# Feed-forward products of a two-block transformer kernel: two 256-column products of the rounded weights become one of 512 columns

## The chip, the core and the metric

The kernel runs on one core of one Trainium2 chip. The metric is the device time of one execution in microseconds (us), taken as the median of several runs. TensorE (PE), VectorE (DVE), ScalarE (ACT), GpSimd (POOL) and SyncE (SP) each work through a queue of instructions of their own, in order, and wait for each other by semaphores.

## What is computed

A first block of two layers, and a second block with gated recurrences and a mixture of experts. Only the first block's feed-forwards are touched. There are four of them (two in each of two layers), on 256 tokens of width 1024, with 2816 hidden channels:

```python
def rms_norm(x, g, eps=NORM_EPS):
    xf = x.astype(jnp.float32)
    y = xf * lax.rsqrt(jnp.mean(xf * xf, axis=-1, keepdims=True) + eps)
    return (y * g.astype(jnp.float32)).astype(x.dtype)

def swiglu(x, w_gu, w_down):
    g, u = jnp.split(x @ w_gu, 2, axis=-1)
    return (jax.nn.silu(g) * u) @ w_down
...
    for l in range(DEPTH):
        x = x + 0.5 * swiglu(rms_norm(x, ffn1_norm[l]), ffn1_w_gu[l], ffn1_w_down[l])
        x = x + hybrid_mixer(rms_norm(x, mix_norm[l]), ...)
        x = x + 0.5 * swiglu(rms_norm(x, ffn2_norm[l]), ffn2_w_gu[l], ffn2_w_down[l])
```

Everything is float32. A product of float32 precision is made from three products of a shorter format: a matrix is split into a rounded part and the rest (w = wh + wl, x = xh + xl), and w·x is taken as wl·xh + wh·xl + wh·xh. The fourth term is left out.

## The kernel before

Activations lie transposed: channels in the 128 partitions, the 256 tokens (`T`) in the columns. `mm3` (line 284) issues the three products of one pair of 128x128 weights and 128x256 activations into the same 256 columns of PSUM, each with a weight load of its own.

**The up products** (`ffn`, `tensor`): for each of `NFF` = 22 steps n, the gate and the up half (s = 0, 1) of 128 hidden channels, each over `KD` = 8 slices of x: 16 calls of `mm3`, 48 matmuls. Both halves lie in one PSUM bank of 512 columns, taken from a ring of eight. **The down products**: 12 half-jobs of weights of 256 columns (8, 8, 8, 8, 6, 6 slices of the hidden channels, twice), two output blocks each, 176 calls of `mm3`. So a feed-forward makes 352 + 176 calls, 1584 matmuls.

**The weights** come from HBM by SP's queue into a ring of three slots. For each step n ACT rounds a 128x2048 half of a slot (`wh<-RB`, line 423) and DVE subtracts (`wl<-RB,wh`, line 432). `wh` and `wl` have three places each. The loops of ACT and DVE do this for step n + 2 at the top of their iteration n (`ws.high(n + 3)`, `ws.low(n + 3)`), before what they do with the result of step n. `wh` of step m needs the place of step m - 3, so it waits for up(m - 3).

**Behind up(n)**, in the order written by hand:

- DVE, L812: both halves times 1/rms (`RST`), PSUM to SBUF ("scaled");
- ACT, L776: silu of the gate half in place; then L768, the rounding `hh` of step n - 1;
- POOL, L849: silu times the up half ("hidden");
- DVE, L800: `hl`, the rest of step n - 1.

In one iteration DVE does wl(n+2), scaled(n), hl(n-1), and ACT does wh(n+2), silu(n), hh(n-1). At n = 6, 12 and 18 a product for the second block ("ada") follows the up product on PE, and DVE copies its row (`MR`, L758) at the end of the iteration; at n = 7, 13 and 19 PE turns that row. After the down products of four blocks DVE adds them to x (L834).

At the start PE sums the squares after up(0) and ACT and DVE make 1/rms from them, so scaled(0) is late by these steps. The first feed-forward also has some one-time steps: the exponentials of a scalar (with a table load on ACT) at n = 1, and the angles of the rotary embedding on DVE at n = 4 and 6.

Of the kernel before, what the change touches and what calls it, by code (L numbers as in the profile page):

```python
# [15 lines left out]
T = 256  # L16
DM = 1024
KD = 8
# [203 lines left out]
def program(nc, A, out, known):  # L222
    stack = ExitStack()
    with stack:
# [18 lines left out]
        PS = [stack.enter_context(nc.psum_tensor(f"ps{i}", [128, 512], F32))[:] for i in range(8)]  # L243
# [14 lines left out]
        def ps_of(*product):  # L258
            return PS[bank_of[product]]

# [383 lines left out]
        class Head:  # L644
# [3 lines left out]
            def __init__(self, st, g, source, *free):  # L648
                self.st, self.g, self.source, self.free = st, g, source, free
                self.xh, self.xl = sb("xh" + st, X_HIGH, [KD, T], F32R), sb("xl" + st, X_LOW, [KD, T], F32R)  # L650
# [43 lines left out]
        def ffn(f, ws, head, then):  # L694

            st, xh, xl = f"f{f}", head.xh, head.xl
            hh, hl = sb(f"hh{f}", STAGE, [NFF, T], F32R), sb(f"hl{f}", STAGE + 5632, [NFF, T], F32R)
# [3 lines left out]

            def tensor():
                for n in range(NFF):
                    parts = [ws.weights(n)] if n + f else []
                    ps = bank(("up", f, n), ("scaled", f, n))
                    for s in range(2):
                        for k in range(KD):
                            if n + f == 0 and s == 0 and k in (0, 4):
                                parts.append(ws.first(k // 4))
                            hi, lo = parts[k // 4 if n + f == 0 else 0]  # L710
                            j = 2 * k + s if n + f else 2 * (k % 4) + s
                            PE.wait_ge(*at("x_low", st, k))
                            ins = mm3(ps[:, s * T:(s + 1) * T], (hi[:, j, :], lo[:, j, :]),
                                      (xh[:, k, :], xl[:, k, :]), k == 0, k == KD - 1)
# [6 lines left out]
                for g2 in range(2):  # L721
                    bs = [bank(("down", f, 3 * g2 + 2, i // 2, i % 2), ("added", f, 4 * g2 + i)) for i in range(4)]
                    for j, (k0, nk) in enumerate(((0, 8), (8, 8), (16, 6))):
                        for half in range(2):
                            hi, lo = ws.weights(22 + 2 * (3 * g2 + j) + half)
                            for i in range(2):
                                for k in range(nk):
                                    PE.wait_ge(*at("hid_low", f, k0 + k))
                                    ins = mm3(bs[2 * half + i][:, 0:T],
                                              (hi[:, k, 128 * i:128 * i + 128], lo[:, k, 128 * i:128 * i + 128]),  # L730
                                              (hh[:, k0 + k, :], hl[:, k0 + k, :]), k0 + k == 0, k0 + k == NFF - 1)
# [21 lines left out]
            def ada_dve(i, before):  # L753
                if i is not None:
# [3 lines left out]
                    V.tensor_copy(MR, ps_of("ada", i)).then_inc(*did("ada_row", i))  # L758
                if before is not None:
# [5 lines left out]
            def scalar():  # L765
# [31 lines left out]
            def vector():  # L797
# [9 lines left out]
                for n in range(NFF):  # L807
                    ws.low(n + 3)
                    DV.wait_ge(*at("up", f, n))
                    if n >= 4:  # L810
                        DV.wait_ge(*at("hid_low", f, n - 4))
# [10 lines left out]
                    ada_dve(ada_at(f, n), ada_at(f, n - 1))  # L822
                hidden_low(NFF - 1)
                for g2 in range(2):
                    for j in range(3):
                        for half in range(2):
# [3 lines left out]
                            if j == 2:  # L830
                                for i in range(2):
                                    c = 4 * g2 + 2 * half + i
                                    DV.wait_ge(*at("down", f, 3 * g2 + 2, half, i))
                                    V.scalar_tensor_tensor(out=XT[:, c, :],  # L834
                                                           in0=ps_of("down", f, 3 * g2 + 2, half, i)[:, 0:T], scalar=0.5,
# [3030 lines left out]
```

## Time and profile before

| | |
|---|---|
| median of 3 runs | 2518.46 us (2517.13 to 2522.33) |
| the profiled execution, its own time | 2515.94 us |
| its span | 2514.2 us |
| PE busy, share of the span | 2420.3 us, 96% |
| DVE, ACT, POOL busy | 56%, 47%, 12% |
| share of PE in the chain that ended last | 82% |
| granted clock of TensorE, mean | 0.991 of full speed |

The profiled execution lies 2.5 us below the median, and 1.7 us of its time lie around the span. A matmul's duration in the trace reaches over the next one's start, since matmuls are pipelined; what one costs in a stream is the distance of two starts. A row of the timeline has the start (us), the duration (us), engine, line, operation, out<-in and shape, and in brackets the idle time of the engine just before and what ended it.

### The profile page before, as it was taken

The numbers are of one execution on the slowest core, as the hardware profiler recorded it, in microseconds if no ns is written. First come the engines' busy times: TensorE is split into PE (matmuls) and PEld (weight loads), VectorE is DVE, ScalarE is ACT, GpSimd is POOL, SyncE is SP. The second block draws the span as 40 slices with busy tenths as digits, with TensorE's granted clock in tenths as the row PEclk, the third lists the DMA queues.
The fourth block names the chain that finished last, engine by engine and source line by source line (L and its number), as shares of the span: only waits on it lengthen the run. The fifth ranks groups of instructions, "written<-read, shape, count | busy, mean of one in ns | idle before, by whom it ended". The sixth has DMA issues, their size and how long they took to land.

```text
span 2514.2 us, 52384 instructions
## 1 busy us (share of the span) xinstructions
PE 2420.3 (96%) x23215; PEld 2090.9 (83%) x23215; DVE 1408.3 (56%) x2208; ACT 1194.1 (47%) x1725; POOL 296.4 (12%) x417
## 2 busy tenths in 40 slices
PE   7999999999999999999999999899999888999998
PEld 7999888799999998878899995686477767778887
DVE  5655544366646655543666566563434454378886
ACT  5434465444344444474454346431255342277775
POOL 0100000031101100000301000462133222000000
PEclk9999999999999999999999999999999899999999
DMA  8754522266656755422457622101200111379995
GB/s 255 245 207 152 204 89 93 105 202 213 223 184 202 236 183 182 141 99 103 142 194 235 214 74 101 69 4 39 72 32 4 70 37 42 133 245 366 368 364 179
DMA packets 269173, 396.14 MB, mean 158 GB/s; under 512 B 9353, under 2 KB 172862, under 8 KB 268814
## 3 DMA queue, kind: packets, MB, share of 16 engines
q1 hardware_dynamic: 267209, 389.32, 45.2%
q8 instruction: 185, 3.03, 0.5%
q0 software_dynamic: 1120, 2.17, 0.3%
q10 hardware_dynamic: 612, 1.24, 0.1%
q14 instruction: 47, 0.38, 0.0%
HBM read 391.66 MB, written 1.05 MB: 156 GB/s over the span
## 4 chain that ended last, share of the span: by engine, by line
PE 82%; DVE 6%; DMA 6%; ACT 3%; issue 2%; POOL 0%; SPq 0%; ACTq 0%; DVEq 0%; POOLq 0%
PE ps L282 81%; DMA RB<-in_moe_w_up 5%; DVE gwl L432 2%; ACT gwh L423 1%; DVE wl L432 0%; PE ps L1131 0%; ACT wh L423 0%; DVE AR L642 0%; ACT AR L2883 0%; DVE AT L1216 0%; DVE AR L1952 0%; PE ps L526 0%; ACT AR L2875 0%; ACT AT L1185 0%; DMA VR<-in_diff_gain 0%
## 5 line engine op out<-in xcount | busy, mean ns | idle before, releaser
L432 DVE TENSOR_TENSOR wl<-RB,wh 128x2048 fp32r<-128x2048 f32 (+5 forms) x189 | 412.4, 2186 | 283.2 <-ACT wh L423 282.7
L282 PE MATMUL ps<-H,RB 128*128 128x256 f32 (+2 forms) x1728 | 452.8, 421 | 2.8 <-ACT AR L2854 1.3
L423 ACT ACTIVATE wh<-RB 128x2048 fp32r<-128x2048 f32 (+5 forms) x189 | 342.2, 1815 | 230.9 <-PE ps L282 202.7
L282 PEld LDWEIGHTS ps<-H,RB 128*128 128x128 f32 (+1 forms) x1728 | 320.2, 189 | 114.8 <-issue 76.9
L282 PE MATMUL ps<-xhf,wl 128*128 128x256 f32 x1408 | 402.9, 286 | 3.6 <-DVE xlf L671 3.6
L282 PE MATMUL ps<-xlf,wh 128*128 128x256 f32 x1408 | 399.4, 284 | 0.0
L282 PE MATMUL ps<-xhf,wh 128*128 128x256 f32 x1408 | 399.3, 284 | 0.0
L282 PE MATMUL ps<-AR 64*64 64x64 f32 (+3 forms) x8296 | 262.9, 233 | 43.7 <-issue 27.4
L282 PEld LDWEIGHTS ps<-AR 64*64 64x64 f32 (+2 forms) x8296 | 229.2, 140 | 83.2 <-issue 66.0
L282 PEld LDWEIGHTS ps<-xhf,wl 128*128 128x128 f32 x1408 | 271.1, 193 | 14.3 <-issue 10.1
L282 PEld LDWEIGHTS ps<-xlf,wh 128*128 128x128 f32 x1408 | 271.2, 193 | 0.1
L282 PEld LDWEIGHTS ps<-xhf,wh 128*128 128x128 f32 x1408 | 271.2, 193 | 0.0
L432 DVE TENSOR_TENSOR gwl<-RB,gwh 128x2048 fp32r<-128x2048 f32 x96 | 217.3, 2289 | 37.4 <-ACT gwh L423 35.8
L423 ACT ACTIVATE gwh<-RB 128x2048 fp32r<-128x2048 f32 x96 | 183.3, 1925 | 44.3 <-DMA RB<-in_moe_w_up 30.1
L282 PE MATMUL ps<-hh,wl 128*128 128x256 f32 x704 | 199.2, 283 | 0.0
L282 PE MATMUL ps<-hl,wh 128*128 128x256 f32 x704 | 199.2, 283 | 0.0
L282 PE MATMUL ps<-hh,wh 128*128 128x256 f32 x704 | 199.2, 283 | 0.0
L776 ACT ACTIVATE H<-H 128x256 f32<-128x256 f32 x88 | 36.8, 419 | 294.6 <-DVE H L812 294.6
L282 PEld LDWEIGHTS ps<-hh,wl 128*128 128x128 f32 x704 | 135.2, 192 | 0.0
L282 PEld LDWEIGHTS ps<-hl,wh 128*128 128x128 f32 x704 | 135.2, 192 | 0.0
L282 PEld LDWEIGHTS ps<-hh,wh 128*128 128x128 f32 x704 | 135.2, 192 | 0.0
L1452 POOL TENSOR_TENSOR H<-H 128x256 f32<-128x256 f32 x48 | 47.6, 1027 | 683.6 <-DVE H L1423 683.5
(445 smaller groups left out, 4109.0 us busy)
## 6 DMA issues: line engine op xcount, KB each, us to landing
RB<-in_ffn_w_gu SPq DMA_DIRECT2D x88, 1024.0 KB, 7.7
RB<-in_w_in SPq DMA_DIRECT2D x25, 2048.0 KB, 7.8
RB<-in_ffn_w_down SPq DMA_DIRECT2D x16, 2048.0 KB, 7.8
RB<-in_w_gate SPq DMA_DIRECT2D x16, 2048.0 KB, 8.8
RB<-in_moe_w_gate SPq DMA_DIRECT2D x32, 1024.0 KB, 7.6
RB<-in_moe_w_up SPq DMA_DIRECT2D x32, 1024.0 KB, 10.2
RB<-in_moe_w_down SPq DMA_DIRECT2D x32, 1024.0 KB, 8.2
RB<-in_ada_w SPq DMA_DIRECT2D x12, 2048.0 KB, 9.8
```

Source lines behind the costliest of these rows:

```text
L282: return M.matmul(o, lhsT, rhs, start=start, stop=stop, skip_group_check=True)
L423: S.activation(self.pair(h)[0], of(slot_of(*key)), ACT.Copy).then_inc(*did("high", *mark))
L432: V.tensor_tensor(lo, of(slot_of(*key)), hi.bitcast(F32), ALU.subtract).then_inc(*did("low", *mark))
L776: S.activation(sil[:, n % 4, 0, :], sil[:, n % 4, 0, :], ACT.Silu).then_inc(*did("silu", f, n))
L1452: P.tensor_tensor(HB[:, c, :], HB[:, c, :], tmp[:, (8 * i + c) % 4, :], ALU.add).then_inc(*did("merged", l, br, c))
```

## The change

In the feed-forwards, the two parts of x (and of the hidden channels) lie side by side, [xh | xl], 512 columns for each slice. The three products become two: one of 512 columns past wh, giving wh·xh and wh·xl in the two halves of a bank, and one of 256 columns past wl, added into the right half (wl·xh). The small terms so stand in a bank half of their own, and are added at the end. An up step now needs a pair of banks. The last two output blocks of the down products (second group, second half) stay as they were. So 352 + 132 of the 528 calls in a feed-forward change, 1936 in all four.

On ACT a copy of the two right halves to SBUF is new ("rest"); on DVE the old operation L812 is replaced by two: the addition of the left halves and the copy ("summed"), and the multiplication by 1/rms in SBUF ("scaled"). Their order in an iteration also changes. For the down products DVE adds the right half in an operation of its own ("added_rest").

```diff
+        def two_banks(product, *readers):
+            n = bank_at.get(every_bank, 0)
+            n += n % 2
+            bank_at[every_bank] = n + 2
+            for b in (n % 8, n % 8 + 1):
+                for mark in bank_free[b]:
+                    PE.wait_ge(*at(*mark))
+                bank_free[b] = readers
+            bank_of[product] = n % 8
...
+        def mm3_apart(o, w, x, start, stop):
+            wh, wl = w
+            mm(o, wh, x.rearrange("p h n -> p (h n)"), start, False)
+            return mm(o[:, T:2 * T], wl, x[:, 0], False, stop)
...
+            def apart(g2, half):
+                return (g2, half) != (1, 1)
...
-                    ps = bank(("up", f, n), ("scaled", f, n))
+                    two_banks(("up", f, n), ("summed", f, n))
...
-                            ins = mm3(ps[:, s * T:(s + 1) * T], (hi[:, j, :], lo[:, j, :]),
-                                      (xh[:, k, :], xl[:, k, :]), k == 0, k == KD - 1)
+                            ins = mm3_apart(pair_of("up", f, n)[:, s].rearrange("p h n -> p (h n)"), (hi[:, j, :], lo[:, j, :]),
+                                            x[:, k], k == 0, k == KD - 1)
... scalar():
                     ws.high(n + 3)
+                    AC.wait_ge(*at("up", f, n))
+                    if n >= 4:
+                        AC.wait_ge(*at("hid_low", f, n - 4))
+                    S.activation(sil[:, n % 4], pair_of("up", f, n)[:, :, 1], ACT.Copy).then_inc(*did("rest", f, n))
+                    if n:
+                        hidden_high(n - 1)
                     AC.wait_ge(*at("scaled", f, n))
                     S.activation(sil[:, n % 4, 0, :], sil[:, n % 4, 0, :], ACT.Silu).then_inc(*did("silu", f, n))
-                    if n:
-                        hidden_high(n - 1)
... vector():
                     ws.low(n + 3)
-                    DV.wait_ge(*at("up", f, n))
...
-                    V.tensor_tensor(sil[:, n % 4], ps_of("up", f, n).rearrange("p (s n) -> p s n", s=2),
-                                    RST.unsqueeze(1).broadcast_to([128, 2, T]), ALU.mult).then_inc(*did("scaled", f, n))
+                    DV.wait_ge(*at("rest", f, n))
+                    V.tensor_tensor(sil[:, n % 4], pair_of("up", f, n)[:, :, 0], sil[:, n % 4], ALU.add).then_inc(
+                        *did("summed", f, n))
+                    ada_row(ada_at(f, n))
                     if n:
                         hidden_low(n - 1)
+                    DV.wait_ge(*at("summed", f, n))
+                    V.tensor_tensor(sil[:, n % 4], sil[:, n % 4], RST.unsqueeze(1).broadcast_to([128, 2, T]),
+                                    ALU.mult).then_inc(*did("scaled", f, n))
...
+                                    if apart(g2, half):
+                                        V.scalar_tensor_tensor(out=XT[:, c, :], in0=ps[:, T:2 * T], scalar=0.5,
+                                                               in1=XT[:, c, :], op0=ALU.mult,
+                                                               op1=ALU.add).then_inc(*did("added_rest", f, c))
+                                        DV.wait_ge(*at("added_rest", f, c))
```

The order on DVE in the first feed-forward, before, from the copy of the ada row (n = 6) through iterations 7 and 8. L432 is wl(n+2), L812 scaled(n), L800 hl(n-1), L761 the end of the ada step.

```order
61 L758 COPY MR_509<-ps 128x512 [waits s_ada]
62 L432 TENSOR_TENSOR wl_460<-RB,wh_459 128x2048 [waits s_high]
63 L812 TENSOR_TENSOR H<-ps,SM 128x512 [waits s_hid_low,s_up]
64 L800 TENSOR_TENSOR hl_507<-H,hh_506 128x256 [waits s_hid_high]
65 L761 TENSOR_TENSOR SM<-ps,VEC 128x8 [waits s_turned]
66 L432 TENSOR_TENSOR wl_460<-RB,wh_459 128x2048 [waits s_high]
67 L812 TENSOR_TENSOR H<-ps,SM 128x512 [waits s_hid_low,s_up]
68 L800 TENSOR_TENSOR hl_507<-H,hh_506 128x256 [waits s_hid_high]
69 L432 TENSOR_TENSOR wl_460<-RB,wh_459 128x2048 [waits s_high]
```

The same iterations 7 and 8 on DVE after the change. L454 is wl(n+2), L848 summed(n), L838 hl(n-1), L854 scaled(n), L795 the end of the ada step.

```order
69 L454 TENSOR_TENSOR wl_460<-RB,wh_459 128x2048 [waits s_high]
70 L848 TENSOR_TENSOR H<-ps,H 128x512 [waits s_rest]
71 L838 TENSOR_TENSOR hid_504<-H,hid_504 128x256 [waits s_hid_high]
72 L854 TENSOR_TENSOR H<-H,SM 128x512 [waits s_summed]
73 L795 TENSOR_TENSOR SM<-ps,VEC 128x8 [waits s_turned]
74 L454 TENSOR_TENSOR wl_460<-RB,wh_459 128x2048 [waits s_high]
75 L848 TENSOR_TENSOR H<-ps,H 128x512 [waits s_rest]
76 L838 TENSOR_TENSOR hid_504<-H,hid_504 128x256 [waits s_hid_high]
77 L854 TENSOR_TENSOR H<-H,SM 128x512 [waits s_summed]
```

Two operations (L848, L838) now stand between wl and the operation that silu waits for, where none stood before.

The order on ACT, before: L423 is wh(n+2), L776 silu(n), L768 hh(n-1).

```order
54 L423 ACTIVATE wh_459<-RB 128x2048 [waits s_up]
55 L776 ACTIVATE H<-H 128x256 [waits s_scaled]
56 L768 ACTIVATE hh_506<-H 128x256 [waits s_hidden]
57 L423 ACTIVATE wh_459<-RB 128x2048 [waits s_up,s_ring1]
58 L776 ACTIVATE H<-H 128x256 [waits s_scaled]
59 L768 ACTIVATE hh_506<-H 128x256 [waits s_hidden]
```

And after: L445 is wh(n+2), L812 now the new copy "rest"(n), L802 hh(n-1), L816 silu(n), L591 a sine of the first feed-forward.

```order
54 L445 ACTIVATE wh_459<-RB 128x2048
55 L812 ACTIVATE H<-ps 128x512 [waits s_hid_low,s_up]
56 L802 ACTIVATE hid_504<-H 128x256 [waits s_hidden]
57 L816 ACTIVATE H<-H 128x256 [waits s_scaled]
58 L591 ACTIVATE SM<-SM 128x16 [waits s_dve_once]
59 L445 ACTIVATE wh_459<-RB 128x2048 [waits s_ring0]
```

The rounding of step n - 1 has moved from behind silu(n) to ahead of it, and the next wh follows silu directly.

## Rows read from the trace of the kernel before

**Rows 1.** Page, parts 1 and 4: busy time of engines; chain by line.

```profile
PE 2420.3 (96%) x23215; PEld 2090.9 (83%) x23215; DVE 1408.3 (56%) x2208; ACT 1194.1 (47%) x1725; POOL 296.4 (12%) x417
...
PE ps L282 81%; DMA RB<-in_moe_w_up 5%; DVE gwl L432 2%; ACT gwh L423 1%; DVE wl L432 0%; PE ps L1131 0%; ACT wh L423 0%; DVE AR L642 0%; ACT AR L2883 0%; DVE AT L1216 0%; DVE AR L1952 0%; PE ps L526 0%; ACT AR L2875 0%; ACT AT L1185 0%; DMA VR<-in_diff_gain 0%
```

**Rows 2.** Timeline, PE, second feed-forward: first down products, 29 matmuls apart.

```profile
688.43 0.28 PE L282 MATMUL ps<-hh,wl 128*128 128x256 f32 x1
...
691.91 0.28 PE L282 MATMUL ps<-hh,wh 128*128 128x256 f32 x1
```

**Rows 3.** Timeline, PE, projection of 512 columns, 20 matmuls apart.

```profile
259.70 0.39 PE L282 MATMUL ps<-wl,xhp 128*128 128x512 f32 x1
...
264.23 0.39 PE L282 MATMUL ps<-wh,xlp 128*128 128x512 f32 x1
```

**Rows 4.** Timeline, DVE, second feed-forward, iteration 5 and the start of 6.

```profile
588.64 2.29 DVE L432 TENSOR_TENSOR wl<-RB,wh 128x2048 fp32r<-128x2048 f32 x1 [1.05 <-ACT wh L423]
590.85 0.68 DVE L812 TENSOR_TENSOR H<-ps,SM 128x512 f32<-128x512 f32 x1
592.33 0.76 DVE L800 TENSOR_TENSOR hl<-H,hh 128x256 fp32r<-128x256 f32 x1 [0.79 <-ACT hh L768]
594.13 2.29 DVE L432 TENSOR_TENSOR wl<-RB,wh 128x2048 fp32r<-128x2048 f32 x1 [1.04 <-ACT wh L423]
596.34 0.69 DVE L812 TENSOR_TENSOR H<-ps,SM 128x512 f32<-128x512 f32 x1
```

**Rows 5.** Timeline, ACT, the same stretch.

```profile
591.57 0.42 ACT L776 ACTIVATE H<-H 128x256 f32<-128x256 f32 x1 [2.96 <-DVE H L812]
591.89 0.40 ACT L768 ACTIVATE hh<-H 128x256 fp32r<-128x256 f32 x1
592.20 1.90 ACT L423 ACTIVATE wh<-RB 128x2048 fp32r<-128x2048 f32 x1
```

**Rows 6.** Timeline, POOL, the same stretch.

```profile
592.06 0.74 POOL L849 TENSOR_TENSOR H<-H 128x256 f32<-128x256 f32 x1 [4.75 <-ACT H L776]
```

**Rows 7.** Timeline, DVE, second feed-forward, two iterations further on (L812 alone).

```profile
662.67 0.69 DVE L812 TENSOR_TENSOR H<-ps,SM 128x512 f32<-128x512 f32 x1 [0.17 <-PE ps L282]
...
668.42 0.69 DVE L812 TENSOR_TENSOR H<-ps,SM 128x512 f32<-128x512 f32 x1 [0.17 <-PE ps L282]
```

**Rows 8.** Timeline, DVE, second feed-forward: scaled(0), then wl of step 3.

```profile
563.50 0.68 DVE L812 TENSOR_TENSOR H<-ps,SM 128x512 f32<-128x512 f32 x1
566.47 2.29 DVE L432 TENSOR_TENSOR wl<-RB,wh 128x2048 fp32r<-128x2048 f32 x1 [2.29 <-ACT wh L423]
```

**Rows 9.** Timeline, DVE: two operations back to back, three times.

```profile
71.44 0.68 DVE L758 COPY MR<-ps 128x512 f32<-128x512 f32 x1
72.05 2.28 DVE L432 TENSOR_TENSOR wl<-RB,wh 128x2048 fp32r<-128x2048 f32 x1
...
187.18 0.75 DVE L834 SCALAR_TENSOR_TENSOR XT<-ps,XT 128x256 f32<-128x256 f32 x2
```

**Rows 10.** Groups by form, DVE: an operation of 512 columns with SBUF operands only.

```profile
L2948 DVE TENSOR_TENSOR AR<-AR 128x512 f32<-128x512 f32 x8 | 5.5, 683 | 0.0
```

**Rows 11.** Timeline, DVE, the end of the second feed-forward's up part.

```profile
691.08 0.43 DVE L800 TENSOR_TENSOR hl<-H,hh 128x256 fp32r<-128x256 f32 x1 [0.20 <-ACT hh L768]
692.88 2.29 DVE L432 TENSOR_TENSOR wl<-RB,wh 128x2048 fp32r<-128x2048 f32 x1 [1.37 <-ACT wh L423]
```

**Rows 12.** Timeline, ACT, the same place: silu of step 21, then the next wh.

```profile
689.35 0.42 ACT L776 ACTIVATE H<-H 128x256 f32<-128x256 f32 x1 [3.23 <-DVE H L812]
...
690.96 1.89 ACT L423 ACTIVATE wh<-RB 128x2048 fp32r<-128x2048 f32 x1
```

**Rows 13.** Timeline, first feed-forward: wl of steps 3 and 4; first down product.

```profile
34.55 2.29 DVE L432 TENSOR_TENSOR wl<-RB,wh 128x2048 fp32r<-128x2048 f32 x1 [2.29 <-ACT wh L423]
...
41.96 2.29 DVE L432 TENSOR_TENSOR wl<-RB,wh 128x2048 fp32r<-128x2048 f32 x1 [1.59 <-ACT wh L423]
...
159.72 0.28 PE L282 MATMUL ps<-hh,wl 128*128 128x256 f32 x1
```

More of the change, by code:

```diff
@@ L242, in program @@
         EPS = SM[:, 400:402]
-        PS = [stack.enter_context(nc.psum_tensor(f"ps{i}", [128, 512], F32))[:] for i in range(8)]
+        PAIRS_OF_BANKS = [stack.enter_context(nc.psum_tensor(f"ps{i}", [128, 1024], F32))[:] for i in range(4)]
+        PS = [PAIRS_OF_BANKS[i // 2][:, 512 * (i % 2):512 * (i % 2) + 512] for i in range(8)]
         bank_at, bank_free, bank_of = {}, [()] * 8, {}
@@ L259, in ps_of, with pair_of @@
             return PS[bank_of[product]]
+        def two_banks(product, *readers):
[7 more added lines that the diff above has]
+            bank_of[product] = n % 8
+        def pair_of(*product):
+            return PAIRS_OF_BANKS[bank_of[product] // 2].rearrange("p (s h n) -> p s h n", s=2, h=2)
         def view(tensor, col, *dims):
@@ L728, in tensor @@
                                     PE.wait_ge(*at("hid_low", f, k0 + k))
-                                    ins = mm3(bs[2 * half + i][:, 0:T],
-                                              (hi[:, k, 128 * i:128 * i + 128], lo[:, k, 128 * i:128 * i + 128]),
-                                              (hh[:, k0 + k, :], hl[:, k0 + k, :]), k0 + k == 0, k0 + k == NFF - 1)
+                                    w = hi[:, k, 128 * i:128 * i + 128], lo[:, k, 128 * i:128 * i + 128]
+                                    if apart(g2, half):
+                                        ins = mm3_apart(bs[2 * half + i], w, hid[:, k0 + k], k0 + k == 0,
+                                                        k0 + k == NFF - 1)
+                                    else:
+                                        ins = mm3(bs[2 * half + i][:, 0:T], w, (hh[:, k0 + k, :], hl[:, k0 + k, :]),
+                                                  k0 + k == 0, k0 + k == NFF - 1)
                                 ins.then_inc(*did("down", f, 3 * g2 + j, half, i))
@@ L751, in ada_pe, with ada_row @@
                     ins.then_inc(*did("turned", "ada", before))
-            def ada_dve(i, before):
+            def ada_row(i):
                 if i is not None:
@@ L758, in ada_dve, with ada_mod @@
                     V.tensor_copy(MR, ps_of("ada", i)).then_inc(*did("ada_row", i))
+            def ada_mod(before):
                 if before is not None:
@@ L833, in vector @@
                                     DV.wait_ge(*at("down", f, 3 * g2 + 2, half, i))
-                                    V.scalar_tensor_tensor(out=XT[:, c, :],
-                                                           in0=ps_of("down", f, 3 * g2 + 2, half, i)[:, 0:T], scalar=0.5,
+                                    ps = ps_of("down", f, 3 * g2 + 2, half, i)
+                                    if apart(g2, half):
+                                        V.scalar_tensor_tensor(out=XT[:, c, :], in0=ps[:, T:2 * T], scalar=0.5,
+                                                               in1=XT[:, c, :], op0=ALU.mult,
+                                                               op1=ALU.add).then_inc(*did("added_rest", f, c))
+                                        DV.wait_ge(*at("added_rest", f, c))
+                                    V.scalar_tensor_tensor(out=XT[:, c, :], in0=ps[:, 0:T], scalar=0.5,
                                                            in1=XT[:, c, :], op0=ALU.mult,
```

12 lines of the change are left out of this document (6 added, 6 removed).

## The prediction

> **What bounds the kernel now.** I read the page's busy times and chain first [rows 1]: PE is busy for 96% of the span, and 81% of the chain that ended last are its matmuls of line 282. So I asked what a feed-forward costs on PE, and then, from the timelines of DVE and ACT, how far these are from being the bound themselves.
>
> In a stream of 256-column products, 29 starts take 691.91 - 688.43 = 3.48 us, 120 ns each [rows 2]. In a stream of 512 columns 20 starts take 4.53 us, 226.5 ns each [rows 3]. So a matmul has a part of about 13.5 ns that does not grow with its columns (240 - 226.5). An up step has 48 matmuls, 5.76 us on PE. Late in the up part that is what is seen: the two L812 stand 5.75 us apart, and DVE was idle for 0.17 us until PE was done [rows 7].
>
> Early in it the distance is another: 596.34 - 590.85 = 5.49 us, with no wait for PE [rows 4]. Here DVE and ACT hold each other in a **cycle**, which starts to start reads: wl to scaled 2.21, scaled to silu 0.72, silu to hh 0.32, hh to the next wh 0.31, wh to wl 1.93: 5.49 [rows 4, 5]. It is closed because both queues are in order: wh(n+3) stands behind silu(n) on ACT, and scaled(n+1) behind wl(n+3) on DVE. The cycle is 0.27 us shorter than PE's step, so after the late start by 1/rms DVE catches up. That is the narrow margin that matters here: of a step's 5.76 us the shares "DVE 56%, ACT 47%" show nothing.
>
> **The change, PE's part.** A changed call takes 226.5 + 120 = 346.5 ns, in place of 360: 13.5 ns less. 1936 of them are 26.1 us. An up step would take 16 x 0.3465 = 5.54 us.
>
> The bounds of this term: 0 (the mixed stream of 512 and 256 columns stands nowhere in the trace; the fixed part may belong to other things) and 26.1 us. I take 13.5 ns, since both lengths show the same fixed part. The Trainium skill ("TensorE: Matmul & The Clock Gate", Back-to-back issue gap) gives N/2.4 + 2.5 ns for an isolated gap, 109 ns at 256 and 216 ns at 512; by it a call would save 2.5 ns only. The trace has 120 and 226.5, so it does not agree.
>
> **The change, the cycle.** On DVE, in place of one operation ahead of silu, there are three: summed (512 columns, PSUM and SBUF like L812), hl (256), scaled (512, SBUF only). An operation of 512 columns takes 0.69 us from PSUM and 0.68 from SBUF alone [rows 4, 10], and the next can start 0.61 after it (72.05 - 71.44) [rows 9]. Two of 256 columns take 0.75, so one costs 0.33 to the next start [rows 9].
>
> hl took 0.76 (592.33) [rows 4]. But that is with POOL's multiplication beside it, which started 0.27 earlier [rows 5, 6]; where POOL was idle it took 0.43 [rows 11]. Now hl(n-1) stands behind summed(n), some 4 us after POOL's work for n - 1, so I take the short one, 0.34 to the next start. The Trainium skill ("SBUF — State Buffer", SBUF: two separate sides) says that a VectorE instruction with two SBUF inputs and a GpSimd instruction lock each other out for the whole instruction; by that rule, too, the new scaled (now two SBUF inputs) is safe only because POOL is idle then, and the trace's 0.76 against 0.43 agrees.
>
> On ACT, hh now precedes silu, and the next wh follows silu after 0.32. The copy "rest" is new, but it stands behind wh(n+2), beside wl(n+2): it starts 1.8 after wh, it must be done 1.93 + 2.21 = 4.14 after wh, and an ACT operation on four times its columns takes 1.90 [rows 5]. So I cost it at nothing, as hh, which is also there. If that cover went, each would add its length, at most 1.9.
>
> The new cycle: wl to summed 2.21, summed to hl 0.61, hl to scaled 0.34, scaled to silu 0.72, silu to wh 0.32, wh to wl 1.93: **6.13 us**. That is longer than PE's step, old or new. Its bounds: 5.8 (summed and scaled together cost one 0.61 and hl nothing more than a wait's 0.3) and 6.5 (hl stays at 0.68 to the next start).
>
> So in the up part PE will wait for its weights, about 6.13 - 5.54 = 0.59 us at most of the steps, and what it gained is spent. The cycle does not wait for PE, since wh(n+2) only needs up(n-1), done long before. So I follow the cycle alone from the start, to the place where PE is free of it again.
>
> **Second to fourth feed-forward** (their rows are the same to 0.01 us in distance). Before: wl(3) starts at 566.47 [rows 8], the down products at 688.43 [rows 2], 121.96 later. The first two half-jobs are 32 calls x 0.36 = 11.52, so the third starts 133.48 after wl(3).
>
> After, counted from the same zero:
> - scaled(0) waits for summed(0): + 0.75 (0.68 and some 0.07 to hand over).
> - up(0) is 16 x 13.5 ns = 0.22 shorter, and with it the sum, 1/rms and all that follows: - 0.22.
> - wl(3) to wl(23): 20 cycles, 122.6. At n = 3 ACT has 0.2 us of other work on the cycle, and at n = 6, 12 and 18 the ada row's copy now stands ahead of scaled, 3 x 0.61 = 1.83.
> - wl(23) to wl(24), where the up part ends: 2.21 + 0.61 + 0.34 + 0.72, then silu(21) to wh(24), 1.61, with POOL between [rows 12], and 1.92 to wl(24) [rows 11, 12]: 7.41.
> - wl takes 2.29, and PE starts 0.05 later: 2.34.
>
> The sum is 134.91: the third half-job starts 1.43 later than before. From there DVE and ACT have two operations of 2 us for each 5.5 us of PE, and PE is the bound again. Of the 132 changed down calls 100 lie behind this place: - 1.35. Each of the three: **+ 0.1 us**.
>
> **First feed-forward.** Before, wl(3) to the down products is 159.72 - 34.55 = 125.17 [rows 13], 3.21 more than in the others, by the one-time steps. Of these, 1.92 are the table load and the exponential on ACT, between silu and wh (41.96 - 34.55 = 7.41, less 5.49); they stay on the cycle. The rest is the angles on DVE, behind hl; in the new order DVE would idle there for wh, and I let them keep 0.1. So the new sum has 2.0 where the old had 3.2, and up(0) runs at the low clock and gains nothing (+ 0.2): about **- 1.0 us**.
>
> **What else moves.** One more addition on DVE for each of six of the eight output blocks (0.34 each) lies in DVE's idle time; the last two blocks, on which the next stage waits, are unchanged. The pairs of banks: an up step needs those of 3 or 4 steps ago (2 steps, next to an ada step), freed at summed; at that place PE waits for the ada row anyway. SP's queue: a slot comes free with wl, later than before, but no faster than DVE asks for it. I cost these at nothing.
>
> Sum: 3 x 0.1 - 1.0 = - 0.7 us on 2515.9. The profiled execution is 2.5 us below the median, so the median would be 2517.8: **no change**. A measurement of this kernel can tell about 0.2% (5 us) from no change. 80 cycles hang on my 6.13: each 0.06 us of error in it makes 5 us, so the forecast's own range is 6.03 to 6.23, 2510 to 2526.
>
> **Rivals.**
> 1. *PE stays the bound*, since DVE's new work fits beside ACT's: then 26.1 us are gained, 2492. For it: DVE is idle by 1.0 and 0.8 us in each iteration [rows 4]. Against: this idle time is the wait for wh and hh, inside the cycle. It would need a cycle below 5.54.
> 2. *Part of it*: the new pair of operations costs less than 1.2 us, the cycle is 5.8 to 6.0, 10 to 26 us less work than mine over 80 cycles, cut where PE becomes the bound: 2496 to 2507.
> 3. *Slower, by hl and POOL*: hl stays at its 0.76, 0.68 to the next start [rows 4]. The cycle is 6.47, and 80 x 0.34 = 27 us are added: 2545. It decides as soon as the cycle is above 6.19 (5 us). Against: POOL's work of step n - 1 is over some 4 us before. Smaller additions at the handovers (0.1 in each cycle, 8 us, 2526) belong here.
> 4. *The change does not do what it says on PE*: the mixed stream saves nothing, or 2.5 ns a call as by the page above. In the up part this changes nothing, as the cycle is the bound; the down part loses 400 x 13.5 ns = 5.4 us of gain and up(0) 0.7: 2524.
>
> **Chances**: the forecast 0.60, rival 1 0.09, rival 2 0.12, rival 3 0.14 (half of it the small kind), rival 4 0.05. Faster by over 0.2%: rivals 1 and 2, and 0.07 of the forecast's: 0.28. Slower: rival 3, most of 4, and 0.06 of the forecast's: 0.24. Within 0.2%: 0.48. The range, with no more than 2 in 10 left out: 2504 to 2530.
>
> **What would show it.** In the profile after: starts of a 512 and a 256-column product 346 ns apart as a pair; in the second feed-forward the L432 for wl (then line 454) 6.13 us apart from the first steps to the last, hl at 0.43; PE idle for some 0.6 us in most up steps, put down to wl; the third half-job of the down products about 1.4 us later, counted from wl(3). Wrong if wl's starts come at 5.54 to 5.76 with DVE waiting for the copy "rest" (rival 1), if hl stays at 0.76 (rival 3), or if PE has no idle time in the up part.

## The result and the profile after

The changed kernel takes 2525.07 us (median of 20 runs, 2517.65 to 2528.73), the kernel before 2517.09 (20 runs, 2511.45 to 2522.59): a ratio of 1.003, 95% interval 1.0021 to 1.0038. So it is **slower by 0.3%, some 8 us**; I had forecast no change, 2517.8, with a range of 2504 to 2530. The profiled execution of the change took 2524.01 us, its span is 2522.3.

Page of the changed kernel, parts 1 and 4, against [rows 1]:

```profile
PE 2418.7 (96%) x21279; PEld 1990.8 (79%) x21279; DVE 1431.4 (57%) x2320; ACT 1235.4 (49%) x1813; POOL 297.0 (12%) x417
...
PE 60%; DVE 20%; ACT 10%; DMA 6%; issue 3%; POOL 0%; SPq 0%; ACTq 0%; DVEq 0%
PE ps L297 59%; DVE wl L454 9%; ACT wh L445 7%; DMA RB<-in_moe_w_up 5%; DVE gwl L454 2%; DVE H L854 2%; DVE H L848 2%; DVE hid L838 1%; ACT gwh L445 1%; PE ps L1176 0%; ACT H L816 0%; DVE AR L664 0%; DVE MR L790 0%; DVE AT L1261 0%; DVE AR L1997 0%
```

PE runs 1936 matmuls fewer and is busy for only 1.6 us less. This number hides both what PE gained and what it now waits: a record's duration reaches over the next start, so it also covers a part of the wait behind it. The starts shown below tell more. The chain is another: PE's matmuls carry 59% of it and no longer 81%; wl, wh, summed and scaled carry 20%. That is the cycle of the prediction. Here it is in the timeline of DVE, second feed-forward, against [rows 4]:

```profile
585.85 2.29 DVE L454 TENSOR_TENSOR wl<-RB,wh 128x2048 fp32r<-128x2048 f32 x1 [2.49 <-ACT wh L445]
...
591.97 2.29 DVE L454 TENSOR_TENSOR wl<-RB,wh 128x2048 fp32r<-128x2048 f32 x1 [2.29 <-ACT wh L445]
594.18 0.68 DVE L848 TENSOR_TENSOR H<-ps,H 128x512 f32<-128x512 f32 x1
594.78 0.42 DVE L838 TENSOR_TENSOR hid<-H,hid 128x256 fp32r<-128x256 f32 x1
595.11 0.68 DVE L854 TENSOR_TENSOR H<-H,SM 128x512 f32<-128x512 f32 x1
598.08 2.29 DVE L454 TENSOR_TENSOR wl<-RB,wh 128x2048 fp32r<-128x2048 f32 x1 [2.29 <-ACT wh L445]
```

and on ACT, against [rows 5]:

```profile
595.83 0.42 ACT L816 ACTIVATE H<-H 128x256 f32<-128x256 f32 x1 [3.11 <-DVE H L854]
596.15 1.90 ACT L445 ACTIVATE wh<-RB 128x2048 fp32r<-128x2048 f32 x1
597.95 0.58 ACT L812 ACTIVATE H<-ps 128x512 f32<-128x512 f32 x1
```

wl to summed 2.21, to hl 0.60, to scaled 0.33, to silu 0.72, to wh 0.32, to wl 1.93: 6.11 us, where 6.13 was forecast. hl took 0.42. PE waits for wl (timeline of PE, the end of one step and the start of the next, twice):

```profile
581.39 0.28 PE L297 MATMUL ps<-xf,wl 128*128 128x256 f32 x1
581.88 0.50 PE L297 MATMUL ps<-xf,wh 128*128 128x512 f32 x1 [0.21 <-DVE wl L454]
...
587.52 0.28 PE L297 MATMUL ps<-xf,wl 128*128 128x256 f32 x1
588.20 0.50 PE L297 MATMUL ps<-xf,wh 128*128 128x512 f32 x1 [0.40 <-DVE wl L454]
```

Within a step the next start follows such a 256-column product after 0.12 us. Here it follows after 0.49 and 0.68, so 0.37 and 0.56 us are lost, where the brackets show 0.21 and 0.40. The prediction had some 0.6.

**Where the 8 us came from.** I cut each profiled execution into stages by the first matmul of each on PE. The table is in us; the last column runs from the last feed-forward's end to the end of the span, the second block, whose source the change does not touch. The experiments below are cut in the same way.

| execution | ffn 1 | mixer 1 | ffn 2 | ffn 3 | mixer 2 | ffn 4 | second block |
|---|---|---|---|---|---|---|---|
| before | 205.96 | 326.43 | 202.29 | 202.28 | 326.46 | 204.04 | 1029.63 |
| before, again | 204.87 | 328.12 | 202.28 | 202.29 | 326.46 | 204.03 | 1026.84 |
| changed | 204.67 | 328.15 | 202.48 | 202.95 | 328.16 | 204.70 | 1034.32 |

The four feed-forwards together take 814.80 us, against 814.57 in the first row and 813.48 in the second, so 0.2 to 1.3 us more, where 0.7 less was forecast. What is longer lies **outside them**: 1.7 us in a mixer, or in two, and 5 to 7 us in the second block. The mixers are told quickly. In the windows of the changed kernel, TensorE's granted clock is below 1.00 at one place of each, for part of 8 us; this is the one in the first mixer (columns: stretch, length, PE, PEld, DVE, ACT, POOL busy with instructions, granted clock, DMA share, GB/s):

```profile
328.00:332.00 4.00, 3.42 (x13) 2.68 (x14) 1.61 (x6) 1.71 (x2) 0.00 (x0) 0.79 0.00 0
332.00:336.00 4.00, 4.00 (x15) 3.06 (x15) 0.00 (x0) 0.54 (x3) 0.00 (x0) 0.78 0.00 0
```

The same stretches of the first execution of the kernel before, where the mixer starts 1.5 us later, and of its second one (0.4 us later):

```profile
328.00:332.00 4.00, 2.99 (x21) 2.49 (x20) 2.11 (x5) 0.71 (x2) 0.00 (x0) 1.00 0.02 4
332.00:336.00 4.00, 4.00 (x20) 3.27 (x19) 1.02 (x3) 2.20 (x4) 0.00 (x0) 1.00 0.00 0
```

```profile
328.00:332.00 4.00, 3.02 (x12) 2.36 (x13) 1.73 (x6) 1.31 (x2) 0.00 (x0) 0.83 0.00 0
332.00:336.00 4.00, 4.00 (x15) 3.07 (x14) 0.29 (x1) 0.54 (x2) 0.00 (x0) 0.75 0.00 0
```

The levels are 2.4 GHz (1.00) and 1.2 GHz (0.50), so 0.79 is a stretch in which the clock was low for 40% of the time. PE is idle for 0.6 us of the first of the two windows (busy for 3.42 of 4.00), and no less where the clock stays at 1.00 (2.99). The kernel before has this fall in one execution and not in the other, and pays the same 1.7 us (326.43 against 328.12). So in the first mixer it comes and goes from one execution to the next. In the second mixer I saw it only in changed kernels, and there in two of eight profiles. The second block is another matter: in the change and in two of its variants (experiments 1 and 3) it took 1034.2 to 1036.7 us, in three profiles with the feed-forwards of before (experiments 1 and 2 among them) 1026.2 to 1029.6, and its instructions and their order are the same. The experiments had to find that.

### The profile page after: what moved, and what is told of

The parts are those of the page before. It is cut to its first block, busy times and chain, and to the rows that moved or that the text cites. A ratio compares the mean times of both kernels' runs of the same rounds, so it can differ in the third digit from the quotient of the medians.

```text
span 2522.3 us, 48667 instructions
## 1 busy us (share of the span) xinstructions
PE 2418.7 (96%) x21279; PEld 1990.8 (79%) x21279; DVE 1431.4 (57%) x2320; ACT 1235.4 (49%) x1813; POOL 297.0 (12%) x417
## 4 chain that ended last, share of the span: by engine, by line
PE 60%; DVE 20%; ACT 10%; DMA 6%; issue 3%; POOL 0%; SPq 0%; ACTq 0%; DVEq 0%
PE ps L297 59%; DVE wl L454 9%; ACT wh L445 7%; DMA RB<-in_moe_w_up 5%; DVE gwl L454 2%; DVE H L854 2%; DVE H L848 2%; DVE hid L838 1%; ACT gwh L445 1%; PE ps L1176 0%; ACT H L816 0%; DVE AR L664 0%; DVE MR L790 0%; DVE AT L1261 0%; DVE AR L1997 0%
## 5 line engine op out<-in xcount | busy, mean ns | idle before, releaser
L454 DVE TENSOR_TENSOR wl<-RB,wh 128x2048 fp32r<-128x2048 f32 (+5 forms) x189 | 411.7, 2185 | 356.4 <-ACT wh L445 356.0
L297 PE MATMUL ps<-xf,wh 128*128 128x512 f32 x1408 | 504.0, 402 | 6.2 <-DVE xf L694 3.7
L445 ACT ACTIVATE wh<-RB 128x2048 fp32r<-128x2048 f32 (+5 forms) x189 | 341.4, 1814 | 208.4 <-PE ps L297 181.1
L297 PE MATMUL ps<-xf,wl 128*128 128x256 f32 x1408 | 394.9, 280 | 0.0
L297 PEld LDWEIGHTS ps<-xf,wh 128*128 128x128 f32 x1408 | 265.0, 188 | 84.6 <-DVE wl L454 11.6
L297 PEld LDWEIGHTS ps<-xf,wl 128*128 128x128 f32 x1408 | 266.3, 189 | 0.1
L297 PE MATMUL ps<-hid,wh 128*128 128x512 f32 (+1 forms) x880 | 249.5, 352 | 5.4 <-DVE wl L454 5.4
L454 DVE TENSOR_TENSOR gwl<-RB,gwh 128x2048 fp32r<-128x2048 f32 x96 | 217.3, 2290 | 37.3 <-ACT gwh L445 35.8
L445 ACT ACTIVATE gwh<-RB 128x2048 fp32r<-128x2048 f32 x96 | 183.3, 1926 | 44.3 <-DMA RB<-in_moe_w_up 30.2
L297 PE MATMUL ps<-hid,wl 128*128 128x256 f32 x704 | 195.9, 281 | 0.0
L297 PE MATMUL ps<-wh,xp 128*128 128x512 f32 (+3 forms) x640 | 177.6, 361 | 0.7 <-DVE wl L454 0.7
L297 PEld LDWEIGHTS ps<-hid,wh 128*128 128x128 f32 x880 | 153.2, 189 | 30.4 <-DVE wl L454 6.9
L816 ACT ACTIVATE H<-H 128x256 f32<-128x256 f32 x88 | 36.8, 418 | 275.3 <-DVE H L854 275.3
L297 PEld LDWEIGHTS ps<-hid,wl 128*128 128x128 f32 x704 | 133.2, 189 | 0.5
L297 PEld LDWEIGHTS ps<-wh,xp 128*128 128x128 f32 x640 | 114.7, 188 | 19.1 <-DVE wl L454 1.5
```

What stands on the lines that cost most here:

```text
L297: return M.matmul(o, lhsT, rhs, start=start, stop=stop, skip_group_check=True)
L445: S.activation(self.pair(h)[0], of(slot_of(*key)), ACT.Copy).then_inc(*did("high", *mark))
L454: V.tensor_tensor(lo, of(slot_of(*key)), hi.bitcast(F32), ALU.subtract).then_inc(*did("low", *mark))
```

## The experiments

Each was timed beside the kernel before on the same chip, whose median there was 2514.13 us for experiments 1 to 3, 2514.91 for 4, and 2512.57 for 5 and 6. A ratio compares with these executions; it can differ by 0.1% from the quotient of the two medians.

### 1 and 2. The kernel before again; the next weight's high half ahead of the wait, in both kernels

The kernel before, unchanged, tells what one execution differs from the next by. And the cycle is tested by a single moved line. In `ffn`, `scalar`, of the changed kernel:

```
                     if n:
                         hidden_high(n - 1)
+                    ws.high(n + 4)
                     AC.wait_ge(*at("scaled", f, n))
```

In the kernel before the same line stands ahead of the same wait, behind a wait for up(n).

> The kernel before, unchanged, profiled once more. Theory A (the half-clock stretches of TensorE outside the feed-forwards lie at fixed places of a given kernel, since they hang on how its sparse stretches of matmuls fall): the stretch at 326 to 346 us of the span again shows a granted clock of 1.00, and the time is 2517 within 3 us. Rival B (their places change from execution to execution): the stretches of half clock lie elsewhere than in the first profile, at about 8 of 17 places or more, and the time of a single execution scatters by 5 us and more to both sides.

> The changed kernel with one thing moved: on ACT the rounding of the weights of step n+3 is issued ahead of silu(n), where it waits for nothing that DVE makes. Theory (the cycle over DVE and ACT bounds the up part): wl no longer waits for the silu, PE is the bound, the up part of each feed-forward is about 6.5 us shorter (16 calls x 13.5 ns x 22 steps = 4.8 us that PE gained, and the 1.4 us by which the third half-job of the down products was late), 26 us in all: 2499 us, the starts of a step 5.54 us apart and no wait for wl. Rival (PE itself does not run the mixed stream faster in the long run, or DVE is too full): steps stay above 5.76 us and the time above 2515 us.

> The same move in the kernel before: the rounding of step n+3 ahead of silu(n) on ACT. Theory (there PE was the bound for most of each up part and the cycle of 5.49 us never held it up): no change beyond the scatter, 2515 to 2520 us. Rival (the order on ACT is worth something for itself): 2500 us or less, as in the changed kernel with the same move.

Measured: before again 2513.28 us, ratio 1.0001 (0.9992 to 1.0011). I had expected the granted clock at 326 to 346 us to be 1.00 again. It was not (0.83 and 0.75 above), so these falls are not at fixed places of a kernel. The moved line in the changed kernel: **2501.08 us, 0.9939 (0.9924 to 0.9954)**. In the kernel before: 2514.18 us, 0.9998 (0.9989 to 1.0007). One line is worth over 20 us in the changed kernel and nothing in the other, so the link wh behind silu holds the changed up part, and did not bound the old one. DVE in the changed kernel with the line moved, second feed-forward:

```profile
616.94 2.29 DVE L454 TENSOR_TENSOR wl<-RB,wh 128x2048 fp32r<-128x2048 f32 x1 [0.49 <-ACT wh L445]
620.37 0.69 DVE L849 TENSOR_TENSOR H<-ps,H 128x512 f32<-128x512 f32 x1 [1.14 <-ACT H L812]
...
622.48 2.29 DVE L454 TENSOR_TENSOR wl<-RB,wh 128x2048 fp32r<-128x2048 f32 x1 [0.48 <-ACT wh L445]
```

and its ACT:

```profile
619.74 0.60 ACT L812 ACTIVATE H<-ps 128x512 f32<-128x512 f32 x1 [2.53 <-PE ps L297]
```

The steps are now 5.54 us apart, PE's own time, and DVE waits for the copy "rest", which waits for PE. The feed-forwards took 200.75, 197.08, 197.07 and 198.82 us, 5.2 less than before in each. But this execution's second block took 1036.74 us, so part of the gain was lost again there, as in the changed kernel.

### 3. hl behind scaled on DVE

```
-                    ada_row(ada_at(f, n))
-                    if n:
-                        hidden_low(n - 1)
                     DV.wait_ge(*at("summed", f, n))
                     V.tensor_tensor(sil[:, n % 4], sil[:, n % 4], RST.unsqueeze(1).broadcast_to([128, 2, T]),
                                     ALU.mult).then_inc(*did("scaled", f, n))
+                    ada_row(ada_at(f, n))
+                    if n:
+                        hidden_low(n - 1)
```

> The changed kernel with the operations of DVE in another order: summed, scaled, then the ada row's copy, then hl. scaled then waits 0.72 us for summed in place of 0.95, so the cycle is 2.21 + 0.72 + 0.72 + 0.32 + 1.93 = 5.90 us in place of 6.12, and the copy is off it. Theory of the cycle: 20 cycles x 0.22 + 3 x 0.61 = 6.2 us less in each feed-forward, but not below PE's own step of 5.54: some 4 to 6 us each, 16 to 24 us in all, 2501 to 2509 us. Rival (hl beside POOL's multiplication is stretched to 0.76 us and that matters): hl at 0.76 us, the cycle still 5.90, since hl lies beside ACT's work then. If the cycle is not the bound: no change, 2525 us.

Measured: 2509.84 us, 0.998 (0.9971 to 0.9989), so just above the expected 2501 to 2509; the four feed-forwards give 15.5 us back, where 16 to 24 were expected. DVE, same stretch:

```profile
585.89 2.29 DVE L454 TENSOR_TENSOR wl<-RB,wh 128x2048 fp32r<-128x2048 f32 x1 [1.96 <-ACT wh L445]
588.10 0.68 DVE L848 TENSOR_TENSOR H<-ps,H 128x512 f32<-128x512 f32 x1
588.82 0.69 DVE L851 TENSOR_TENSOR H<-H,SM 128x512 f32<-128x512 f32 x1
589.42 0.42 DVE L838 TENSOR_TENSOR hid<-H,hid 128x256 fp32r<-128x256 f32 x1
591.80 2.29 DVE L454 TENSOR_TENSOR wl<-RB,wh 128x2048 fp32r<-128x2048 f32 x1 [1.96 <-ACT wh L445]
```

The cycle is 5.91 us. It fell by 0.21 and not by hl's 0.33, since scaled, now next to the summed that it reads, starts 0.72 after it and not 0.60: the wait between the two costs 0.12. So of hl's 0.33 between them 0.12 had been free.

### 4. The ring of banks

The instructions of the second block are the same in both kernels, but not their waits. `bank` hands out the eight PSUM banks in turn, by a counter that goes on through the whole program. `two_banks` takes two for an up step and rounds up to an even one. So the changed kernel enters the second block at bank 6, where the kernel before enters it at 0 (the mixers at 4 and 2 in place of 5 and 1). There `bank(..., among=others)` and the like take from fixed halves of the same banks by counters of their own. A product of the main ring then waits for whoever read that bank last, and that reader is another in the changed kernel. PE's list of the second block with the counter moved, against the kernel before (- is before, + is with the ring entered at bank 6; the names are the waits of a row):

```
-L282 MATMUL ps<-H,RB 128x256 [waits s_ring2]
+L282 MATMUL ps<-H,RB 128x256 [waits s_gdn_copy,s_ring2]
 L282 MATMUL ps<-H,RB 128x256 x7
...
 L282 MATMUL ps<-AR_14710 128x128 x8
-L282 MATMUL ps<-H,RB 128x256 x16
+L282 MATMUL ps<-H,RB 128x256 [waits s_o_sum]
+L282 MATMUL ps<-H,RB 128x256 x15
```

Two theories were left: A, the shifted banks; B, that all stands at other moments, so that other sparse stretches fall to 1.2 GHz. Four kernels tell them apart.

The changed kernel, and the one of experiment 1, with the counter set back:

```
+            bank_at[every_bank] += ((5, 1)[layer] - bank_at[every_bank]) % 8
             mixer(layer, projected, into_mixer, branched, head)
...
+        bank_at[every_bank] += -bank_at[every_bank] % 8
         experts(block2(then))
```

The kernel before with the counter moved, `bank_at[every_bank] += 6` ahead of `experts(block2(then))`. And the kernel before made 4 us later there, by nine overwritten products in the last feed-forward's row sum:

```
+                for again in range(9 if (st, k) == ("f3", 0) else 0):
+                    mm(ps[:, 0:T], ones, sq[:, 0, :], True, False)
                 ins = mm(ps[:, 0:T], ones, sq[:, k, :], k == 0, k == KD - 1)
```

> The changed kernel with the counter of the bank ring set, ahead of both mixers and of the second block, to the bank at which the kernel before stands there (numbers 5, 1 and 0 of eight; the change leaves it at 4, 2 and 6). The second block's products then lie in the banks, and wait for the marks, that they have in the kernel before. Theory A (shifted banks: block 2 waits for other readers, 5 to 8 us): the stretch from the end of the last feed-forward to the end goes from 1034.3 back to 1026-1030 us, and the time to 2516-2520 us, ratio 1.000 to the kernel before. Theory B (nothing but the moment matters: other sparse stretches fall to half clock): the stretch stays 1033-1037 us and the time 2522-2527 us. The feed-forwards stay as in the changed kernel under both (202-205 us each).

> The kernel before with the bank counter moved on by 6 (that is, back by 2) ahead of the second block, the place at which the changed kernel enters it; nothing else. Theory A (shifted banks): last stretch 1032-1036 instead of 1026-1030 us, time 5 to 8 us over the kernel before (2519-2522). Theory B (moment and clock): within 2 us of the kernel before, last stretch 1026-1030 us.

> The version with ScalarE's next weight half ahead of its wait (2501.1 us) with the bank counter set back as above. Theory A: last stretch 1026-1030 instead of 1036.7 us, time 2492-2496 us, the best so far. Theory B: 2499-2503 us, no change against that version.

> The kernel before with 9 more 256-column 32-bit products on TensorE in the last feed-forward's row sum (overwritten, so the result is the same), about 0.45 us each: everything behind is 4 us later, banks and waits as they were. Theory A (banks): time +4 us (2518), last stretch unchanged at 1026-1030 us. Theory B (the moment decides which sparse stretches run at half clock): the last stretch itself is 5 to 8 us longer too, time +9 to +12 us.

| kernel | time, us | ratio to before, 95% interval | ffn 4 | second block |
|---|---|---|---|---|
| changed, banks back | 2516.17 | 1.0008 (0.9999 to 1.0017) | 204.65 | 1025.63 |
| before, banks moved | 2519.98 | 1.0021 (1.0011 to 1.0031) | 204.34 | 1033.23 |
| wh early, banks back | **2493.35** | **0.9922 (0.9909 to 0.9934)** | 198.82 | 1028.22 |
| before, 4 us later | 2520.82 | 1.0029 (1.0018 to 1.0040) | 207.90 | 1030.18 |

Theory A stands, from both sides: the change without the shift is not told apart from the kernel before, and the shift alone, put into the kernel before, costs it 5.3 us. Over all profiles the second block takes 1023.0 to 1030.2 us in the eight that enter it at bank 0 and 1033.2 to 1036.7 in the four at bank 6. The delay costs its own 3.9 us in the last feed-forward, and leaves the second block near what the kernel before shows (1026.8 and 1029.6 in two executions, 1030.2 here). Its time rose by 5.9 us (interval 4.5 to 10), so some 2 us more than the delay, and above the 2518 expected; these are not explained. So B is not needed for the shift's cost, but 1 to 2 us of it can't be excluded.

The place can be read. PE some 230 us into the second block, kernel before (its second execution):

```profile
1716.25 3.79 PE L282 MATMUL ps<-H,RB 128*128 128x256 f32 x16
1719.97 3.21 PE L282 MATMUL ps<-AR 128*64 128x128 f32 x48
1723.11 7.17 PE L282 MATMUL ps<-H,RB 128*128 128x256 f32 x32
```

the kernel before with the banks moved:

```profile
1716.26 5.28 PE L282 MATMUL ps<-H,RB 128*128 128x256 f32 x16 [0.84 <-ACT AR L2216]
1721.47 3.21 PE L282 MATMUL ps<-AR 128*64 128x128 f32 x48
1727.60 7.17 PE L282 MATMUL ps<-H,RB 128*128 128x256 f32 x32 [2.92 <-DVE AR L2237]
```

the changed kernel:

```profile
1719.67 5.32 PE L297 MATMUL ps<-H,RB 128*128 128x256 f32 x16 [0.84 <-ACT AR L2261]
1724.93 3.21 PE L297 MATMUL ps<-AR 128*64 128x128 f32 x48
1731.06 5.23 PE L297 MATMUL ps<-H,RB 128*128 128x256 f32 x23 [2.92 <-DVE AR L2282]
```

and the changed kernel with the banks back:

```profile
1718.54 3.72 PE L297 MATMUL ps<-H,RB 128*128 128x256 f32 x16
1722.19 3.21 PE L297 MATMUL ps<-AR 128*64 128x128 f32 x48
1725.33 7.17 PE L297 MATMUL ps<-H,RB 128*128 128x256 f32 x32
```

With the ring at bank 6, the first group of gate products waits 0.84 us for ScalarE's copy of a recurrence product (line 2216, 2261 after). The wait lies ahead of the group, so it is not why the group then takes 5.2 us to the next group in place of 3.7. That is the clock. The windows over the group, in the kernel before (second execution) and in the one with the banks moved:

```profile
1716.00:1720.00 4.00, 4.00 (x22) 3.06 (x18) 0.00 (x0) 0.60 (x1) 0.00 (x0) 0.95 0.00 0
1716.00:1720.00 4.00, 3.74 (x10) 3.07 (x11) 0.00 (x0) 0.11 (x1) 0.00 (x0) 0.56 0.00 0
```

In both the granted clock was low just ahead (0.63 and 0.58 in 1712 to 1716). Without the wait it is back at the group's first products, and with it only at the eighth: until then they start 0.43 us apart, and 0.22 us from there. It is no chance of these two executions: from this group's start to the next group's it is 5.2 to 5.6 us in all four profiles at bank 6, and 3.7 to 3.9 in all eight at bank 0. The group of 32 waits 2.92 us for DVE's reading of the recurrence's output (`out_dve`, line 2237, 2282 after), so that 6.13 us lie between its start and that of the group ahead, in place of 3.14. Together that is 0.8 + 1.5 + 3.0 = 5.3 us, the two waits and the longer half clock behind the first. Without the shift neither wait is there: the work is independent of these results, only the bank is shared.

The execution with hl behind scaled and the one with wh early show the same 0.84 and 2.92. In these two the clock also falls behind the second wait; with wh early it was 0.50 in 1712 to 1716, and from the group of 32 to what follows it is 9.9 us in place of 7.1:

```profile
1710.39 9.99 PE L297 MATMUL ps<-H,RB 128*128 128x256 f32 x32 [2.92 <-DVE AR L2283]
```

So the shift's price is partly paid in clock, and that part differs from one execution to the next. The mean granted clock over all timed executions agrees: 0.9891 with only the banks moved (9 executions) and 0.9910 in the kernel before beside it (23).

### 5. The two parts of the change, each alone

The down part alone (up part, DVE's and ScalarE's order as before, no pairs of banks), and the up part alone: `apart` returns `False`, banks set back as above.

> The change's down part alone: 132 of the 176 calls of each feed-forward's down part are a 512-column and a 256-column product with the small terms apart, the up part and DVE's and ScalarE's order in it are those of the kernel before, no pairs of banks (so the bank ring is not shifted). If a changed call saves 13.5 ns also in the down part, where PE is the bound throughout, each feed-forward is 1.8 us shorter, and the time 7.1 us: 2507-2509. If the mixed stream saved only 2.5 ns a call: 1.3 us in all, 2513-2514. If the addition on DVE behind the six blocks was on the path: up to 0.34 us a feed-forward less gain.

> The change's up part alone, with the bank counter set back ahead of the mixers and of the second block (as in the run that gave 2516.2 us); all down calls are three 256-column products. By the prediction's terms (1.43 us later at the third half-job in the second to fourth feed-forward, 0.35 in the first) 4.6 us over the kernel before: 2519-2520. By what the feed-forwards of the changed kernel measured (0.6 us over those before, where 0.1 was forecast) plus the 1.35 us of down calls: 7 to 8 us over, 2522-2523. If the up part were free of the cycle: under the kernel before.

Measured: **down part alone** 2510.03 us beside 2512.57, ratio 0.9996 (0.9985 to 1.0006). I expected 7 us less, and it is 1 to 3: a miss, by the size of one term. Its second and third feed-forward took 201.33 and 201.32 us, 0.96 less than before, where 132 calls by 13.5 ns are 1.78. The starts of its 512-column products show why:

```profile
689.20 0.40 PE L297 MATMUL ps<-hid,wh 128*128 128x512 f32 x1
...
700.51 0.40 PE L297 MATMUL ps<-hid,wh 128*128 128x512 f32 x1
```

32 calls in 11.31 us, 353.4 ns each: 6.6 ns less than 360. The same calls in the changed kernel, second feed-forward:

```profile
706.77 0.39 PE L297 MATMUL ps<-hid,wh 128*128 128x512 f32 x1
...
717.86 0.39 PE L297 MATMUL ps<-hid,wh 128*128 128x512 f32 x1
```

32 calls in 11.09 us, 346.6 ns each, what I had forecast. There are two paces, and a stream keeps one of them over a hundred calls and more.

**The up part alone** took 2518.18 us beside 2512.57, 1.0027 (1.0017 to 1.0037): 5.6 us over, between the forecast's 4.6 and the 7 to 8, nearer to the first. Its second and third feed-forward took 203.65 and 203.67, 1.37 over before; I had 1.43.

### 6. The ring at another place

The best version, but the second block entered at bank 4, by `(4 - bank_at[every_bank]) % 8`.

> The best version so far (2493.4 us) with the second block entered at bank 4 instead of 0; the mixers at the banks they had. If the second block's time hangs on which readers its products meet in the ring, another place gives another time: anything from 5 us less to 8 us more is expected, and a row in which PE waits for ScalarE's or DVE's last reader at 235 to 245 us into the block, as at bank 6. If bank 6 was one bad case among equals: 2492-2496 us.

Measured: 2503.5 us, 0.9958 (0.9945 to 0.9972), 9 us over the best version by the ratios and 10 by the medians, more than the 8 that I had allowed; the second block 1038.38 us. Bank 6 was not the one bad case. At the place of above the first wait is gone, with the longer half clock behind it, and in place of the second another has come:

```profile
1702.11 3.72 PE L297 MATMUL ps<-H,RB 128*128 128x256 f32 x16
1705.76 3.21 PE L297 MATMUL ps<-AR 128*64 128x128 f32 x48
1711.22 2.49 PE L297 MATMUL ps<-H,RB 128*128 128x256 f32 x6 [2.26 <-DVE AR L2304]
```

DVE's operations fall behind those of the best version by 2 to 3 us at 130 us into the block, by another 5 here and by 1 to 2 more at 360. Five of the ring's eight places were not tried; whether one is better than 0 stays open.

## Why the prediction was wrong, and where it was right

**Right, by the rows of after:**
- The cycle: 6.11 us for 6.13, each of its six distances within 0.02. Experiments 1 and 3 cut it at two places, and the time followed.
- hl at 0.42 with POOL idle, where it took 0.76 beside POOL. Rival 3's large kind did not come. The rule of the Trainium skill ("SBUF — State Buffer", SBUF: two separate sides), that a VectorE instruction with two SBUF inputs and a GpSimd one lock each other out, agrees with these two numbers.
- The copy "rest" hidden behind wh: it starts 1.80 after wh, and DVE waits for wh, not for it.
- The third half-job of the down products of the second feed-forward, 1.43 later forecast: it starts 151.77 us into the stage (701.46), before 150.45, so 1.32 later.
- Rival 1's condition, a cycle below 5.54 us, fails in the change and is met when one line is moved. That its time, 2492, is near what the best version takes (2493.35) is partly luck: it had 26.1 us of gain, and the best version gains 20 to 22 (its feed-forwards 5.2 each), beside a kernel before that took 2514.91 there and not 2518.5.
- The first feed-forward, 1.0 us shorter by forecast: 204.67 and, with the banks back, 205.21, against 204.87 to 206.31 in five profiles of the kernel before and its variants. The sign fits, but the scatter is as large as the term.

**Wrong, the size of a term.** "I take 13.5 ns, since both lengths show the same fixed part": a call in the mixed stream takes 353 ns at the one pace and 347 at the other, so it saves 7 to 13 ns. This is why the second to fourth feed-forward come out at +0.6 us each with the slower pace (202.91 with the banks back) and +0.2 with the faster (202.48), for a forecast of +0.1. It is 1 to 2 us in all. So about half of what rival 4 takes away was in it. The row of 512-column products that I had read [rows 3] was a stream of these alone. The rule of the Trainium skill that I had set against the rows ("TensorE: Matmul & The Clock Gate", Back-to-back issue gap), by which I estimate that a call saves 2.5 ns, agrees with neither pace.

**Wrong, and the cause of the sign**: "What else moves ... The pairs of banks ... I cost these at nothing." I had asked only whether an up step finds its pair free. I had not asked where the ring's counter stands at the end of the feed-forwards. The change takes 118 banks more (614 against 496), which moves all that comes after by 6 of 8 places. Two groups of products in the second block then wait for another reader of their bank (0.84 and 2.92 us), and the first wait keeps the clock low for longer. That cost 5.3 us by the one experiment (ratio 1.0021) and, taken out of the change, gave back all but 1 to 2 us of its 8. It could be read before any run, in PE's list of the second block, where rows have other waits than before. I had read only the feed-forwards' part of the list. With this term in the sum, and the call at 7 ns, the forecast would have been -0.7 + 5.3 + 1.5, 6 us over the median of 2518.5 that it started from, some 2524 us.

What stays open: why the stream has two paces; why the shifted ring's waits draw the clock down in one execution more than in another; and whether the change makes the clock fall somewhat more often with the banks back too. Over all timed executions the mean granted clock was 0.9898 there (11 executions) against 0.9910 beside it. But it was 0.9908 against 0.9912 with the up part alone and 0.9894 against 0.9912 with the down part alone, so it is not tied to the changed up part.

## What to carry to other kernels

A ring of buffers that the whole program shares ties every stage to the number that the stages before took. When a change takes another number from it, list the waits of all that follows, not only of the edited part, or set the counter to a fixed place at each stage's start, and try that place as a parameter (9 to 10 us lay between two of them here).

An engine that is busy for 96% of the span need not be the bound of a stage after the change. Two in-order queues that hand to each other form a cycle; add its start-to-start distances, and compare with the bound's time for one step. If the cycle is longer, look for a link that only the order of the queue makes: here wh(n+4) behind the wait for scaled(n), one line, which turned 0.3% slower into 0.8% faster once the banks were set back too.

## What the runs showed of the hardware

- A stream of alternating 512- and 256-column products runs at 346.6 or at 353.4 ns a call, in the same program; the pace changes where the stream is interrupted. In the execution with wh early, calls went at 353 ns up to a pause at 596 us and at 347 behind it.
- On DVE, an operation that reads the result of the one just before it starts 0.72 us after it, one that doesn't 0.60 (588.10 to 588.82, against 594.18 to 594.78).
- In the first mixer the clock's fall to 1.2 GHz for part of 8 us comes in one execution and not in the next of the same program, and costs 1.7 us each time (326.43 against 328.12 for the mixer).
- A short wait can cost more than its length through the clock: behind 0.84 us of it, at a place where the clock was just low, the granted clock was 0.56 in place of 0.95, and 16 products took 5.2 us in place of 3.7. The same wait came with 5.2 to 5.6 us in all four profiles that have it.
